# Sample attention in a hybrid decoder step: dot products on VectorE, or keys and values streamed past zero-padded query windows on TensorE

## The reference

```
def _dilated_gather_sample(q, kv_new, kv_buf, bias_tab, window, dil):
    kv_all = jnp.concatenate([kv_buf, kv_new], axis=1)
    idx = lb + np.arange(t)[:, None] - jj[None, :] * dil      # jj = 0 .. window/dil
    g = kv_all[:, np.maximum(idx, 0)]
    logits = jnp.einsum('bthd,btkhd->bthk', q, g[:, :, :, 0]) * SCALE + bias
    lse = jax.nn.logsumexp(logits, axis=-1)
    o = jnp.einsum('bthk,btkhd->bthd', jnp.exp(logits - lse[..., None]), g[:, :, :, 1])
def _combine_groups(outs, lses):
    alpha = jax.nn.softmax(jnp.stack(lses, axis=0), axis=0)   # over the three groups
    a = jnp.concatenate([o * alpha[i][..., None] for i, o in enumerate(outs)], axis=-2)
```

## Time and profile before

| | us |
|---|---|
| median of 3 runs | 2049.31 |
| profiled execution, whole | 2055.78 |
| its span | 2053.6 |
| TensorE busy | 1678.3 |
| VectorE busy | 1162.0 |
| ScalarE busy | 592.6 |
| GpSimd busy | 694.6 |
| a broadcast of queries (768 KB), from issue to landing | 14.6 |
| a chunk of column weights (1 MB), from issue to landing | 8.5 |

### The profile page before, as it was taken

One profiled execution on the slowest core, in us unless ns is written; L12 is line 12 of the kernel. 1 busy time (PEld: TensorE's weight loads), 2 busy tenths in 40 slices (PEclk: granted clock), 3 DMA queues, 4 the chain that ended last, 5 costly groups with the idle time before them and its releaser, 6 DMA issues.

```text
span 2053.6 us, 16891 instructions
## 1 busy us (share of the span) xinstructions
PE 1678.3 (82%) x5096; PEld 877.2 (43%) x5096; DVE 1162.0 (57%) x2773; ACT 592.6 (29%) x1828; POOL 694.6 (34%) x686
## 2 busy tenths in 40 slices
PE   6985999998788777777789759999887878777777
PEld 4653875543333333223146557655333333332221
DVE  1454038786776776444435331668777767744544
ACT  2231014342333423222322211334333333322222
POOL 2112003455444344334300120244544534443332
PEclk8887699999899989999999858999989999899999
DMA  5598269999999999999947965699999999999997
GB/s 177 212 379 308 85 244 376 420 407 420 421 420 420 420 420 421 420 420 421 421 180 278 379 218 203 242 402 416 417 420 420 419 421 420 420 421 420 421 421 289
DMA packets 104564, 742.25 MB, mean 361 GB/s; under 512 B 14859, under 2 KB 15958, under 8 KB 23704
## 3 DMA queue, kind: packets, MB, share of 16 engines
q0 software_dynamic: 92480, 640.11, 76.2%
q1 hardware_dynamic: 9684, 56.63, 7.4%
q10 hardware_dynamic: 2308, 44.43, 5.7%
HBM read 736.76 MB, written 48.20 MB: 382 GB/s over the span
## 4 chain that ended last, share of the span: by engine, by line
DMA 45%; PE 39%; DVE 9%; ACT 3%; issue 2%; DVEq 1%; ACTq 1%; POOL 0%; SPq 0%; POOLq 0%
DMA arena<-peer_uv,idx 28%; PE bank L1401 17%; DMA qf<-peer_uv,idx 7%; PE bank L1372 6%; PE bank L1268 4%; PE bank L1501 3%; PE bank L1263 3%; PE bank L1487 3%; DMA scores<-qrows 3%; DVE arena L1095 2%; DMA yt<-peer_uv,idx 2%; DMA wring<-peer_uv,idx 2%; DMA wring<-w_col 2%; DMA wring<-w_tok 1%; PE bank L1356 1%
## 5 line engine op out<-in xcount | busy, mean ns | idle before, releaser
L1401 PE MATMUL bank<-arena,diag 128*128 128x512 f32 (+1 forms) x1456 | 708.4, 632 | 169.5 <-ACT diag L697 169.4
L534 POOL DMA_INDIRECT arena<-peer_uv,idx x364 | 397.4, 1092 | 706.1 <-PE bank L1401 463.5
L1095 DVE SCALAR_TENSOR_TENSOR arena<-arena,xn 128x1024 f32<-128x1024 f32 x364 | 441.3, 1225 | 305.5 <-DMA arena<-peer_uv,idx 303.8
L1401 PEld LDWEIGHTS bank<-arena,diag 128*128 128x128 f32 (+1 forms) x1456 | 269.9, 191 | 577.1 <-issue 317.5
L689 ACT ACTIVATE act<-hid 128x2 f32<-128x2 f32 x288 | 58.6, 203 | 882.3 <-DVE arena L1095 542.3
L1401 PE MATMUL bank<-wring,diag 128*128 128x512 f32 (+1 forms) x352 | 174.8, 636 | 41.8 <-ACT diag L697 41.8
L697 ACT ACTIVATE diag<-ident,weight 128x128 f32<-128x128 f32 (+1 forms) x576 | 194.7, 385 | 20.4 <-issue 0.7
L1268 PE MATMUL bank<-xt,wring 128*128 128x288 f32 x512 | 142.9, 438 | 48.8 <-DVE yt L987 29.0
L1401 PE MATMUL bank<-qf,diag 128*128 128x512 f32 (+1 forms) x304 | 149.9, 631 | 40.1 <-ACT diag L697 40.1
L692 ACT ACTIVATE weight<-act,gate 128x1 f32<-128x1 f32 x576 | 138.4, 287 | 20.4 <-issue 0.7
L1095 DVE SCALAR_TENSOR_TENSOR wring<-wring,xn 128x1024 f32<-128x1024 f32 x88 | 106.7, 1224 | 58.1 <-DMA wring<-peer_uv,idx 57.6
(11 more groups left out here) (230 smaller groups left out, 1537.9 us busy)
## 6 DMA issues: line engine op xcount, KB each, us to landing
kvs<-cache_a_kv_w ACTq DMA_DIRECT2D x16, 2044.0 KB, 14.0
wring<-w_col SPq DMA_DIRECT2D x16, 1024.0 KB, 8.5
qf<-cache_rows POOLq DMA_DIRECT2D x24, 576.0 KB, 8.3
wring<-w_tok SPq DMA_DIRECT2D x8, 1408.0 KB, 10.0
arena<-peer_wq SPq DMA_DIRECT2D x10, 1024.0 KB, 9.1
wring<-w_out SPq DMA_DIRECT2D x8, 1024.0 KB, 5.2
kvs<-cache_a_kv_w ACTq DMA_DIRECT2D x16, 508.0 KB, 8.0
scores<-qrows POOLq DMA_DIRECT2D x8, 768.0 KB, 14.6
```

The source lines that it names most:

```text
L534: pool.indirect_dma_start(out=ring[j], out_offset=None, in_=io["peer_uv"], in_offset=bass.IndirectOffsetOnAxis(ap=idx[:, n:n + 1], axis=0) ...
L1095: last = v.scalar_tensor_tensor(out=ring[j][:, 0:D], in0=ring[j][:, 0:D], scalar=1.0, in1=xn[:, i, :], op0=ALU.mult, op1=ALU.mult, accum_o ...
L1401: last = pe.matmul(bank[b0 + half][0:r, :], diag[:, n % 16, 0:r], ring[SLOT_OF[n]][:, D + 512 * half:D + 512 * half + 512], start=False, s ...
```

## The change

The keys' dot products move from VectorE to TensorE, and the sample softmax becomes one over all groups and both kinds of rows at once.

- The host lays keys out transposed (head dimension on partitions): `cache_keys`, beside `cache_values`, in tiles of the same size as before.
- Queries go into windows. A sequence's output rows are 32: token by token for head 0 in the first half and head 1 in the second half of a 32-row block shared by four sequences. `qz` is a zeroed buffer of 2400 columns in which each pair of sequence and token (or, in the near group, each sequence) has a window of 32 columns that is zero but for its own columns. The 32 columns of a window are the weights of a matmul, the 128 cached keys are streamed, and results are added up in 32 rows of one PSUM bank. A sequence takes 9 such matmuls (`sample_keys`). POOL clears the buffer, VectorE fills it (`query_windows`, 6 copies).
- Values go the same way: `pz` holds the turned probabilities in windows, value blocks are streamed (`sample_values`, 9 matmuls for each sequence), and ScalarE copies the result, TensorE turns it back and ScalarE writes it to `yt`.
- The logits are 64 rows x 480 (3 groups x 160). One maximum, one exponential with its sum, and one scaling stand in place of the group-wise softmax, for the sample alone.
- Order. Seven of eight key tiles have a place of their own and are loaded at the start of the stage; the eighth reuses the first's place. Value loads follow each key block's end. `sample_keys` stands before AS, between AS and BS, and before xb0; the sample softmax beside xb0 and gc0; the values between u1 and the mix block. The prompt's softmaxes follow the sample's.
- Gone: the transpose and round trip of q, the eight broadcasts, `key_dots`, the turn of the key sums, the old value block, and VectorE's last addition.

```diff
-        pool.dma_start(kc[:, b % 4], io["cache_rows"][l, b, 0]).then_inc(k_in[b % 4], 16)
+        pool.dma_start(kc[b], io["cache_keys"][l, b]).then_inc(k_in[b], 16)
...
-                for b in range(4):
+                for b in range(NB - 1):
                     load_k(l, b)
+                if l:
+                    pool.wait_ge(xs_ps, 6 * l)
+                pool.memset(flat_xn[:, 0:2400 + NG * 2 * NS], 0.0).then_inc(qz_clear, 1)
...
-                load_q(0)
-                load_q(1)
-                for b in range(NB):
-                    pool.wait_ge(kq_done, NB * l + b + 1)
...
+                pool.wait_ge(key_ps, NB * l + 1)
+                load_k(l, NB - 1)
+                pool.wait_ge(qk_done, 6 * (l + 1))
+                pool.memset(pz, 0.0).then_inc(pz_clear, 1)
+                for b in range(1, NB - 1):
+                    pool.wait_ge(key_ps, NB * l + b + 1)
+                    load_v(l, b)
+                pool.wait_ge(key_ps, NB * (l + 1))
+                load_v(l, 0)
+                load_v(l, NB - 1)
...
+            def query_windows(l):
+                v.drain()
+                v.wait_ge(qz_clear, l + 1)
+                for h in range(2):
+                    r = slice(64 * h, 64 * h + 64)
+                    near = qz[r, 0:8 * 36].rearrange("p (a b w) -> p a b w", a=2, b=4)[:, :, :, 16 * h:16 * h + NT]
+                    v.tensor_copy(near, qt[r, 0, SEQ:TOKENS].rearrange("p (a b t) -> p a b t", a=2, b=4))
+                    far = qz[r, 8 * 36:2400].rearrange("p (g a m w) -> p g a m w", g=2, a=2, m=16)[:, :, :, :, 16 * h]
+                    v.tensor_copy(far, qt[r, 1:3, SEQ:TOKENS].rearrange("p g (a m) -> p g a m", a=2))
...
+            def sample_max(l):
+                v.wait_ge(logit_ps, 3 * l + 1)
+                v.scalar_tensor_tensor(out=lgs[0:2 * NS, :, :], in0=slog, scalar=SCALE, in1=sbias[:, :, :],
+                                       op0=ALU.mult, op1=ALU.add).then_inc(slog_read, 1)
+                v.drain()
+                v.tensor_reduce(smax[0:2 * NS, :], lgs[0:2 * NS, :, :].rearrange("p g n -> p (g n)"), AX.X, ALU.max,
+                                negate=True).then_inc(max_done, 1)
...
+            def sample_keys(l, b):
+                if b == 0:
+                    pe.wait_ge(qz_done, l + 1)
+                pe.wait_ge(k_in[b], 16 * (l + 1))
+                r, near, far = windows_of(qz, b)
+                pe.matmul(slog[r, 0, 0:P], near, kc[b][:, 8, :], start=(b % 4 == 0), stop=False)
+                for t in range(NT):
+                    for g in range(2):
+                        last = pe.matmul(slog[r, g + 1, 0:P], far[g][t], kc[b][:, 4 * g + t, :], start=False, stop=False)
+                last.then_inc(key_ps, 1)
...
+            def sample_values(l, b):
+                pe.wait_ge(v_in[b], 16 * (l + 1))
+                r, near, far = windows_of(pz, b)
+                pe.matmul(pv_ps[r, 0, :], near, vc[b][:, 8, :], start=False, stop=False)
+                for t in range(NT):
+                    for g in range(2):
+                        last = pe.matmul(pv_ps[r, g + 1, :], far[g][t], vc[b][:, 4 * g + t, :], start=False, stop=(b in (0, NB - 1) and t == NT - 1 and g == 1))
...
# TensorE's order
                 out(l, "k1")
-                sample_rows(l, 1)
                 out(l, "k2")
                 qk_mean(l, 3)
                 qk_mean(l, 4)
+                for b in range(0, 3):
+                    sample_keys(l, b)
                 out(l, "AS")
                 qk_mean(l, 5)
+                for b in range(3, 5):
+                    sample_keys(l, b)
                 out(l, "BS")
+                for b in range(5, NB):
+                    sample_keys(l, b)
+                sample_rows(l)
+                new_logits(l)
                 out(l, "xb0")
-                sample_rows(l, 2)
-                new_logits(l)
                 out(l, "gc0")
+                turn_sample_probs(l)
                 logits(l, 1)
...
                 out(l, "u1")
-                values(l, 0, 1)
+                values(l, 1, 1)
+                new_values(l)
+                for b in range(1, 5):
+                    sample_values(l, b)
                 out(l, "u2")
-                turn_probs(l, 1, 0)
+                turn_probs(l, 2, 0)
+                for b in (5, 6, 0, 7):
+                    sample_values(l, b)
...
                 mix(l, 2)
+                turn_sample_values(l)
                 out(l, "gb0")
-                values(l, 1, 0)
+                values(l, 2, 0)
                 out(l, "gb1")
-                pe.wait_ge(kq_summed, l + 1)
...
-                for b in range(NB):
-                    pe.wait_ge(v_in[b], 16 * (l + 1))
-                    r = slice(b * NT, b * NT + NT)
-                    last = pe.matmul(pv_sum[:, 0, :, r], vc[b][:, 8, :], pts[:, 0:2, r], start=True, stop=True)
-                    for t in range(NT):
-                        for g in (1, 2):
-                            n = b * NT + t
-                            last = pe.matmul(pv_sum[:, g, :, n], vc[b][:, 4 * (g - 1) + t, :], pts[:, 2 * g:2 * g + 2, n], start=True, stop=True)
-                last.then_inc(pv_done, 1)
```

More of the change, by code:

```diff
@@ L628, in col_out, with exps @@
                 a.activation(dst, out_bank(name)[0:w, 0:TOKENS], func).then_inc(took_a, 1)
-            def exps(l, slot, n, rows, logits):
+            def exps(l, slot, n, logits):
                 a.wait_ge(max_done, 3 * l + slot + 1)
-                a.activation(share[0:rows, :], dmax[0:rows, :], ACT.Exp)
+                a.activation(share[:, :], dmax[:, :], ACT.Exp)
                 for h in range(HEADS):
-                    last = a.activation(logits[0:rows, h, 0:n], logits[0:rows, h, 0:n], ACT.Exp,
-                                        bias=nmax[0:rows, h:h + 1], accum_out=esum[0:rows, h:h + 1])
+                    last = a.activation(logits[:, h, 0:n], logits[:, h, 0:n], ACT.Exp,
+                                        bias=nmax[:, h:h + 1], accum_out=esum[:, h:h + 1])
@@ L1218, in bias_samples @@
                 pe.wait_ge(bias_wide, HEADS)
[L1219 to L1222 removed]
+                for g in range(NG):
+                    for j in range(2 * NT):
+                        last = pe.matmul(bank[6][0:2 * NS, g * (P + NS):(g + 1) * (P + NS)], relt[:, 2 * g + j // NT, j % NT * 2 * NS:(j % NT + 1) * 2 * NS],
+                                         csample[:, g, j % NT, :], start=(j == 0), stop=(j == 2 * NT - 1))
                 last.then_inc(bias_ps, 1)
@@ L1287, in new_logits @@
             def new_logits(l):
-                pe.wait_ge(qk_done, 6 * (l + 1))
-                for h in (0, 2, 4, 1, 3, 5):
-                    r = slice(64 * (h % 2), 64 * (h % 2) + 64)
-                    last = pe.matmul(new_ps[h % 2][:, h // 2, :], qt[r, h // 2, SEQ:TOKENS], kt[r, h // 2, SEQ:TOKENS], start=True, stop=True)
+                for g in range(NG):
+                    last = pe.matmul(slog[:, g, P:P + NS], qblk[:, g, :], kt[:, g, SEQ:TOKENS], start=False, stop=(g == NG - 1))
@@ L1293, in new_logits, with turn_sample_probs, new_values @@
                 last.then_inc(logit_ps, 1)
+            def turn_sample_probs(l):
+                pe.wait_ge(prob_done, 3 * l + 1)
+                for g in range(NG):
+                    pe.transpose(pts_ps[:, g, :], lgs[0:2 * NS, g, 0:P], ident[0:2 * NS, 0:2 * NS])
+                    last = pe.transpose(ptn_ps[:, g, :], lgs[0:2 * NS, g, P:P + NS], ident[0:2 * NS, 0:2 * NS])
+                last.then_inc(probt_ps, 1)
+            def new_values(l):
+                pe.wait_ge(probt_done, 3 * l + 2)
+                for g in range(NG):
+                    pe.matmul(pv_ps[:, g, :], ptn[0:NS, g, :], kvn[:, 1, g * P:(g + 1) * P], start=(g == 0), stop=False)
@@ L1295, in logits, with turn_sample_values @@
+            def turn_sample_values(l):
+                pe.wait_ge(pv_copied, l + 1)
+                pe.wait_ge(probt_done, 3 * l + 3)
+                for g in range(NG):
+                    last = pe.transpose(pvt_ps[:, g, :], pvs[0:2 * NS, g, :], ident[0:2 * NS, 0:2 * NS])
+                last.then_inc(pvt_done, 1)
             def logits(l, q):
```

267 lines of the change are left out of this document (119 added, 148 removed).

## The result

The changed kernel takes 1999.28 us (median of 4 runs, 1995.78 to 2002.67) against 2051.14 us of the kernel before in the same job (2048.93 to 2054.47): ratio 0.9746, 95% interval 0.9723 to 0.9769. It is 52 us faster; the forecast was 66 faster (1983), and the time lies inside the range of 1966 to 2024.

The account below looks back on a forecast made before the run. The mixer stage's chain of waits, ending in the sample path, was taken as the bound. Layer gains of 34.0 and 32.5 us sum to 66.5, from a median of 2049.3 to 1983; own case 1970 to 2000, with rivals 1966 to 2024.

Parts of the forecast that it names:

- The path: Mixer stage, k2 to output projection: the sample path sets its end; 36.4 us off layer 0, 33.5 off layer 1.
- 0.23 us: Key and value blocks on TensorE: time of one 128x32 matmul with 128 columns, so 16.6 us for each kind a layer.
- Rivals 3 and 4: Key and value blocks: weight loads not hidden, 2014 us, chance 0.07; clock falls to 1.2 GHz, 2126 us, chance 0.04.
- line 1324's 66 ns: 64-wide values whose neighbours run side by side: time a record, giving the lower bound of 0.13 us a new matmul.
- Waits for VectorE and POOL: Query windows ready at 86, wanted at 90.4; sample probabilities ready at 123, wanted at 125.6: no wait of TensorE.
- 6 + 2 us of wait and restart: T1's weight chunk lands last, 6 us late, plus 2 for half clock after it: 8 us a layer (0 to 16).
- 104.5 us: TensorE's sequence from k2's end to the output projection, without a wait for DMA.
- The 112.5: Stretch from k2 to the output projection: 104.5 us of sequence plus 8 of DMA wait and restart.
- the second output-projection chunk: Issued when gb1 ends, sharing the DMA with copy 6 (3.8 MB, 9.3 us together): 3 us a layer (0 to 10).
- the warm start of -2.6 and -2.0: Output projection begins at full clock after dense work: 2.6 us less in layer 0, 2.0 in layer 1.
- Rival 2: Weight chunks starve in the mixer stage, 29.7 us of waits and restarts a layer against 11: 2021 us, chance 0.19.
- k1's chunk in layer 0, +2: Seven key loads instead of four go out beside the k1/k2 weight chunk, delaying it: 2 us, at most 4.

Follow-up runs that it names:

- b1: Kernel before the change, with six of the eight query broadcasts of a layer left out: 2016.35 us, ratio 0.9829.
- b2: Kernel before the change, with 62 of the 72 sample value matmuls of a layer left out: 1999.82 us, ratio 0.9761.
- p1: Changed kernel, with key and value matmuls of sequences in different halves of the 64 output rows alternating: 1964.54 us, ratio 0.9579.
- e1: Changed kernel, with cache copies 4, 5 and 6 issued between u1 and the mix block instead of beside gb0 and gb1: 1976.71 us, ratio 0.9644.
- e2: Changed kernel, with cache copies 1 and 2 issued after T1 instead of beside xb0 and xb1: 1971.92 us, ratio 0.9618.
- e3: Changed kernel, with all eight value loads issued only at gc1's end, copies left in place: 1986.67 us, ratio 0.9695.
- e5: Changed kernel, with each of the 72 value matmuls of a layer issued twice: 2027.48 us, ratio 0.9894.
- p4: Changed kernel, with p1's alternating matmuls, copies 1 to 3 after T1 and 4 to 6 between u1 and the mix block: 1950.93 us, ratio 0.9523.
- p5: p4 with cache copy 6 issued only at the start of the PEER queries: 1931.27 us, ratio 0.9429.

## Why the prediction was right, and where it was off

**The path.** That the whole sample path (broadcasts, last dots, softmax, old value block) sets the end of the stage, and that all of it goes, was right: 36.8 and 31.3 us came off the stretch, forecast 36.4 and 33.5. b1 and b2 show the two largest pieces of it apart.

**The matmuls.** 0.23 us was taken from AS's 303 ns; measured 1.97 us a block of nine, 0.219 each, 15.8 us for keys and as much for values, at clock 1.00. Rivals 3 and 4 are out: no weight load shows (the block's records follow at 109 ns, near the 108 that 128 columns ask for by the rate of the 288-column records, 243 ns), and the clock stays at 1.00 in both kinds of blocks. The argument for 0.23, the same 32 output rows, was also right, and its reverse is p1's gain. The prediction had the row for that (line 1324's 66 ns) and used it only as a bound.

**Waits for VectorE and POOL.** TensorE had none before the keys or the sample turns, as forecast. The memset of 2592 columns took 2.28 us where 2.7 was reckoned.

**T1.** Forecast 6 + 2 us of wait and restart, measured 10.4 + 1.8 and 11.2 + 3.3. The chunk took 21.4 us, so last place behind the rest was right. From 111 to its landing at 145.4 the queues moved 13.7 MB at 398 GB/s, where 13.1 at 410 and a landing at 143 were reckoned (the sum was near, its parts were not: three copies with 8.2 MB were issued in that time and not two, and less of the value loads was left), and T1 was wanted at 135.0 instead of 136.8: together the 4.2 us by which the forecast wait was too short in layer 0. It was balanced by a sequence that came to 99.9 us instead of 104.5: 1.7 us of that are the key and value blocks, some 0.6 gb0 (5.8 against 6.4), the rest small blocks whose merged records overlap and were added whole. The 112.5 was met in layer 0 by two errors of some 4.5 us each that cancel, which is luck. In layer 1 they were 6.5 and 4.3 (the sequence took 100.2) and left 2.2.

**The step that failed: the second output-projection chunk, "3 us a layer (0 to 10)".** The time lies in the stated range, but the gain fell short by this term. Measured: 8.1 us of wait and 3.0 of restart (6.91 against 3.88) in layer 0, 7.75 + 2.15 in layer 1: 11.1 and 9.9. With the warm start of -2.6 and -2.0, which was right, that gives, within 0.2 us, the 8.7 and 8.1 by which the stretch grew. The gain was 14.6 us short of the forecast, and this term alone is 15.0 over both layers; the smaller misses of the other terms nearly cancel. The working summed the chunk and copy 6 to 3.8 MB and 9.3 us, and it fails in two places. Copy 5, issued 4.9 us before, was still on the queues: at 247 GB/s it can have moved 1.2 of its 2.74 MB by 200.3, so 1.5 MB were ahead, and the next chunk (1 MB) was issued before this one landed. And the queues moved 329 GB/s here, not 410: 5.8 MB in 17.7 us. The chunk landed behind the copies, as T1's had, which the prediction believed there and not here. The restart at half clock, counted for T1 in the same prediction, was left out here. Rival 2 priced the chunk rightly (9.8 and a restart), had T1 8.3 us late, nearer to the 10.4 and 11.2 than the forecast's 6, and missed only with its waits at xb1 and u1, which did not come. In waits and restarts it had 29.7 us a layer and the forecast 11; measured were 23.3 and 24.4. On the waits the rival was nearer, and the forecast of the time was kept near by its sequence, which was too long. e1 shows the term alone: 21.0 us of its 23 came off the two output projections.

**k1's chunk in layer 0, +2.** No wait; 0.

The Trainium skill (DMA: Bandwidth & Descriptors, Queues, rings and completion order) says that each DMA engine takes turns among the queues at packet granularity. By an estimate from that, with turns of equal size, the 1 MB of w_out beside ScalarE's copies would have had half the bandwidth and landed in about twice e1's 4.9 us. The runs show 17.7, and this trace shows packets of unequal size on the two queues. The DMA queues from 195 to 218 us, first the copies' and then that of SP's chunks (packets, MB, share of the engines):

```profile
q10 hardware_dynamic: 224, 5.48, 67.2%
q1 hardware_dynamic: 225, 1.70, 22.3%
```

A packet of the copies had 24.5 KB, one of the weights 7.6. Equal turns of packets would then give the chunk about a quarter of the bytes. That this is the whole cause is argued and not shown, since no run varied the packets.

## What to carry to other kernels

When a long wait goes from a chain, look at every transfer whose cover it was. A chunk that was issued 45 us ahead of its use is now issued 10 ahead, and its price is not its own bytes but most of what is on the queues at that instant, plus a restart at half clock. Transfers that nobody in the kernel waits for should stand where no chunk is about to be issued, and they have to be placed again after each change of the stage: the same move was worth -27 us in one kernel and +11 in the other. And where two matmuls write different 32-row groups, alternate them.

## What was not expected of the hardware

- A 1 MB chunk issued by SP just ahead of a 2.74 MB copy issued by ScalarE landed behind it (17.7 against 16.3 us). w_out took 16.9 to 18.0 us in the six kernels in which copies 5 and 6 were both under way in both layers (after, e2, e3, e5, p1, p4), 7.9 and 10.7 in p5 with copy 6 moved away, and 4.9 and 4.8 without a copy (e1).
- 128x32 matmuls of 128 columns in 32 bits: 0.219 us each in the same 32 output rows, 0.22 us a pair in different ones, both at clock 1.00.
- The wait of 7.8 to 8.1 us in the output projection costs 2.2 to 3.0 us more behind it: the next 16 records took 6.0 to 6.9 us against 3.9, and the granted clock was 0.50 (1.2 GHz) from 215 to 222 us, in the wait's end and the first half of these records.
